# Dilated attention of a two-layer decoder trunk: one run of 64 steps per layer in place of two runs of 32

## What is computed

```python
def _dilated_attention(q, k, v):             # patterns (128, 1), (512, 4), (2048, 16)
    for window, dilation in DILATED_PATTERNS:
        o_i, lse_i = _dilated_branch(qp, kp, vp, window, dilation)
    ...
    w = jax.nn.softmax(jnp.stack(lses, axis=0), axis=0)
    o = jnp.einsum('gbsh,gbshd->bshd', w, jnp.stack(outs, axis=0).astype(jnp.float32))
...
mix = jnp.concatenate([attn, u], axis=-1)    # u: convolution of 31 taps, layernorm, silu
x = x + mix @ w_out[layer]
```

## Time and profile before

| | |
|---|---|
| median of 3 runs | 2617.43 us (2616.72 to 2618.36) |
| span of the profiled execution | 2619.3 us; the page gives no other time for it |
| PE, busy | 2491.9 us (95%) |
| DVE, busy | 1601.5 us (61%) |
| ACT, busy | 792.5 us (30%) |
| POOL, busy | 188.1 us (7%) |

### The profile page before, as it was taken

How to read it: one execution, slowest core, us unless ns; L and a number is a source line. 1 busy time by engine, 2 the same in 40 slices (tenths; PEclk the granted TensorE clock), 3 DMA queues, 4 the chain that set the end, 5 groups by cost and what they waited for, 6 DMA issues and landing times.

```text
span 2619.3 us, 33211 instructions
## 1 busy us (share of the span) xinstructions
PE 2491.9 (95%) x11824; PEld 2064.4 (79%) x11824; DVE 1601.5 (61%) x1490; ACT 792.5 (30%) x1037; POOL 188.1 (7%) x71
## 2 busy tenths in 40 slices
PE   6999889999999999999989997889999999999998
PEld 5878678778888888888778776787788888888887
DVE  5788867454555555555548897664465555555555
ACT  4222355333222222222332224553332222222221
POOL 1223100110000000000002330001100000000000
PEclk8999889999999999999989998999999999999999
DMA  3232631011111111111002226300111111111111
GB/s 120 63 90 72 177 89 48 24 41 49 49 49 48 48 48 48 48 48 48 32 34 73 80 80 185 89 24 32 41 49 48 48 48 48 48 48 48 48 48 72
DMA packets 46379, 159.29 MB, mean 61 GB/s; under 512 B 7392, under 2 KB 7776, under 8 KB 46304
## 3 DMA queue, kind: packets, MB, share of 16 engines
q1 hardware_dynamic: 45152, 154.12, 18.7%
q10 hardware_dynamic: 1152, 4.19, 0.4%
HBM read 133.12 MB, written 25.17 MB: 60 GB/s over the span
## 4 chain that ended last, share of the span: by engine, by line
PE 72%; DVE 13%; DVEq 7%; issue 3%; ACT 2%; DMA 1%; SPq 1%; ACTq 0%
PE mm L397 44%; PE aux L397 19%; DVE y L964 7%; PE aux L536 4%; PE aux L520 2%; DVEq L966 2%; PE mm L500 2%; DVE y L1118 1%; DVEq L1008 1%; DVEq L1120 1%; PE aux L421 1%; PE aux L573 1%; DVE o L1006 1%; DVEq L1001 1%; ACT x_hi L670 1%
## 5 line engine op out<-in xcount | busy, mean ns | idle before, releaser
L397 PE MATMUL mm<-x_hi,w_hi 128*128 128x512 f32 x2304 | 727.3, 397 | 34.7 <-DVE x_lo L937 17.0
L397 PE MATMUL mm<-x_lo,w_hi 128*128 128x512 f32 x2304 | 718.3, 393 | 0.0
L397 PE MATMUL mm<-x_hi,w_lo 128*128 128x512 f32 x2304 | 718.3, 393 | 0.0
L397 PEld LDWEIGHTS mm<-x_hi,w_hi 128*128 128x128 f32 x2304 | 434.9, 190 | 132.4 <-DVE x_lo L937 19.4
L397 PEld LDWEIGHTS mm<-x_lo,w_hi 128*128 128x128 f32 x2304 | 437.4, 190 | 96.1
L397 PEld LDWEIGHTS mm<-x_hi,w_lo 128*128 128x128 f32 x2304 | 436.6, 189 | 93.9
L647 ACT ACTIVATE w_hi<-w_raw 128x1024 fp32r<-128x1024 f32 x188 | 197.2, 1058 | 767.7 <-PE mm L397 576.2
L1133 DVE TENSOR_TENSOR x<-x,aux 128x1024 f32<-128x1024 f32 x176 | 214.8, 1220 | 136.4 <-PE aux L397 126.9
L931 DVE TENSOR_TENSOR w_lo<-w_raw,w_hi 128x1024 fp32r<-128x1024 f32 x188 | 228.2, 1222 | 38.3 <-ACT w_hi L647 25.1
L964 DVE SCALAR_TENSOR_TENSOR y<-u_pad,cpar,y (+1 forms) x152 | 210.8, 1387 | 26.2 <-issue 26.2
L943 DVE TENSOR_TENSOR uv<-mm,rinv 128x1024 f32<-128x1024 f32 x44 | 53.9, 1225 | 220.8 <-PE mm L397 220.5
(11 more groups left out here) (152 smaller groups left out, 2493.9 us busy)
## 6 DMA issues: line engine op xcount, KB each, us to landing
w_raw<-weights SPq DMA_DIRECT2D x188, 512.0 KB, 3.3
qk_scratch<-m SPq DMA_DIRECT2D x64, 128.0 KB, 2.1
qk_scratch<-o SPq DMA_DIRECT2D x64, 128.0 KB, 2.1
x_hi<-qk_scratch SPq DMA_DIRECT2D x32, 256.0 KB, 6.0
x<-xT ACTq DMA_DIRECT2D x8, 512.0 KB, 11.2
q_st<-qk_scratch SPq DMA_DIRECT2D x8, 512.0 KB, 3.5
k_hh<-qk_scratch SPq DMA_DIRECT2D x16, 256.0 KB, 5.7
k_ll<-qk_scratch SPq DMA_DIRECT2D x16, 256.0 KB, 6.1
```

Source lines behind the costliest of these rows:

```text
L397: last = pe.matmul(acc[:, cols], a, b[:, cols], start=start and n == 0, stop=stop and n == 2)
```

## The change

`STEPS` becomes `HEADS * TB` = 64, the loops over `i` go on all four engines, and the eight heads of a layer follow each other without a break. The fills are made for the whole layer: 104 in place of 2 x 52. Output turns come in steps 22, 38, 54 and 70 (`O_AT = 22`), in which they follow the attend of step n - 3; the first three lie in block 6 of heads 2, 4 and 6, where VectorE has no tap. In the output turn ScalarE now copies a bank twice, to `x_hi` and back over the half of `o_nat` that was just transposed, and the second copy frees the bank. VectorE waits for the bank's count and subtracts from that copy in `rinv`. The 44 taps are one list: six in each of heads 0 to 6 and two in head 7. SyncE fetches the values of pairs 2 and 3 at the starts of heads 4 and 6.

```diff
-TURN_HEADS = 4
-TURNS = HEADS // TURN_HEADS
-STEPS = TURN_HEADS * TB
+STEPS = HEADS * TB
+O_AT = 22
...
-    for n in range(STEPS + 6):
+    for n in range(STEPS + 7):
...
-        if n >= 21 and (n - 21) % (2 * TB) == 0:
+        if n >= O_AT and (n - O_AT) % (2 * TB) == 0:
             for half in range(2):
-                fills.append((n, "o", (n - 21) // (2 * TB), half, None))
+                fills.append((n, "o", (n - O_AT) // (2 * TB), half, None))
...
-                with sp.Fori(0, TURNS - 1) as i:
-                    for h in range(2, TURN_HEADS + 2):
-
-                        sp.wait_ge(mm_full, at(l, MM, M_SCORE + (h - 1) * TB, STEPS, i))
-                        load_head(h % 2, i * TURN_HEADS + h)
-                        if h >= TURN_HEADS:
-                            b = h - TURN_HEADS
-                            sp.wait_ge(step_done, at(l, HEADS * TB, (b + 1) * 2 * TB, STEPS, i))
-                            load_v(b, i * 2 + 2 + b)
...
+                for h in range(2, HEADS):
+
+                    sp.wait_ge(mm_full, at(l, MM, M_SCORE + (h - 1) * TB))
+                    load_head(h % 2, h)
+                    if h % 2 == 0 and h >= PAIRS:
+                        pair = h // 2
+                        sp.wait_ge(step_done, at(l, STEPS, (pair - 1) * 2 * TB))
+                        load_v(pair % 2, pair)
...
-                with pe.Fori(0, TURNS) as i:
...
-                with act.Fori(0, TURNS) as i:
...
-                            act.activation(x_hi[:, i * 2 + which, a * BANK:(a + 1) * BANK], bank, ACT.Copy
-                                           ).then_inc(o_hi, 1)
...
+                        act.activation(x_hi[:, which, a * BANK:(a + 1) * BANK], bank, ACT.Copy).then_inc(o_hi, 1)
+                        act.activation(o_nat[:, a * 4:(a + 1) * 4, :], bank.rearrange("p (b c) -> p b c", c=P),
+                                       ACT.Copy).then_inc(pt_read[f % 2], 1)
...
-                with dve.Fori(0, TURNS) as i:
...
-                        dve.wait_ge(o_hi, at(l, 2 * PAIRS, 2 * which + a + 1, 4, i))
-                        out = (slice(None), i * 2 + which, slice(a * BANK, (a + 1) * BANK))
-                        dve.tensor_tensor(x_lo[out], bank, x_hi[out].bitcast(F32), ALU.subtract
-                                          ).then_inc(pt_read[f % 2], 1)
-                        dve.drain().then_inc(o_split, 1)
...
+                    fills = [g for g in range(f + 1) if g % 2 == f % 2]
+                    dve.wait_ge(pt_read[f % 2], at(l, PT // 2, len(fills) + 1))
+                    out = (slice(None), which, slice(a * BANK, (a + 1) * BANK))
+                    dve.tensor_tensor(x_lo[out], rinv[:, a * BANK:(a + 1) * BANK], x_hi[out].bitcast(F32),
+                                      ALU.subtract)
+                    dve.drain().then_inc(o_split, 1)
...
-                    attn_taps = [(c, j) for c in range(CT // TURNS) for j in TAPS_ATTN]
+                attn_taps = [(c, j) for c in range(CT) for j in TAPS_ATTN]
```

More of the change, by code:

```diff
@@ L486, in _ @@
                 plain(pe)
-                with pe.Fori(0, TURNS) as i:
[L488 to L533, removed]
-                        out = stat_s[:, hh * BANK + qb * HEAD_DIM:hh * BANK + (qb + 1) * HEAD_DIM]
-                        for kb in range(qb + 1):
-                            last = pe.matmul(out, pT[n % 2][:, kb, :], vp[b][:, kb, hh * HEAD_DIM:(hh + 1) * HEAD_DIM],
-                                             start=kb == 0, stop=kb == qb)
-                        last.then_inc(step_done, 1)
-                    for n in range(STEPS + 6):
-                        if n < STEPS:
-                            scores(n)
-                        for f in range(PT_TURN):
-                            if FILLS[f][0] == n and FILLS[f][1] == "p":
-                                turn(f)
-                        if 3 <= n < STEPS + 3:
-                            attend(n - 3)
-                        for f in range(PT_TURN):
-                            if FILLS[f][0] == n and FILLS[f][1] == "o":
-                                turn(f)
@@ new lines, in scores @@
+                def scores(n):
+                    h, qb = n // TB, n % TB
+                    b = h % 2
+                    if qb == 0:
+                        pe.wait_ge(head_loaded[b], at(l, 80 * HEADS // 2, 80 * (h // 2 + 1)))
+                    pe.wait_ge(mm_read, at(l, MM, M_SCORE + n + 1))
+                    keys = (qb // 2 + 1) * 2 * P
+                    for a in range(0, keys, BANK):
+                        z = min(a + BANK, keys)
+                        for k in (k_hh, k_ll):
+                            last = pe.matmul(mm[n % 2][:, a:z], q_st[b][:, qb * P:(qb + 1) * P], k[b][:, a:z],
+                                             start=k is k_hh, stop=k is k_ll)
+                    last.then_inc(mm_full, 1)
@@ new lines, in attend @@
+                def attend(n):
+                    h, qb = n // TB, n % TB
+                    b, hh = h // 2 % 2, h % 2
+                    if n % (2 * TB) == 0:
+                        pe.wait_ge(v_loaded[b], at(l, 16 * PAIRS // 2, 16 * (h // 4 + 1)))
+                    if qb == 0:
+                        pe.wait_ge(o_read, at(l, HEADS, h + 1))
+                    for bank in range(2):
+                        fills = [f for f in range(LAST_FILL[n] + 1) if f % 2 == bank]
+                        pe.wait_ge(pt_read[bank], at(l, PT // 2, len(fills) + 1))
+                    out = stat_s[:, hh * BANK + qb * HEAD_DIM:hh * BANK + (qb + 1) * HEAD_DIM]
+                    for kb in range(qb + 1):
+                        last = pe.matmul(out, pT[n % 2][:, kb, :], vp[b][:, kb, hh * HEAD_DIM:(hh + 1) * HEAD_DIM],
+                                         start=kb == 0, stop=kb == qb)
+                    last.then_inc(step_done, 1)
@@ L553, in out_unit @@
+                for n in range(STEPS + 7):
+                    if n < STEPS:
+                        scores(n)
+                    for f in range(PT):
+                        if FILLS[f][0] == n and FILLS[f][1] == "p":
+                            turn(f)
+                    if 3 <= n < STEPS + 3:
+                        attend(n - 3)
+                    for f in range(PT):
+                        if FILLS[f][0] == n and FILLS[f][1] == "o":
+                            turn(f)
                 def out_unit(u, k0, midway=None):
```

155 lines of the change are left out of this document (83 added, 72 removed).

## The result

| | before | after |
|---|---|---|
| median, us | 2617.07 (2615.45 to 2618.36, 4 runs) | 2599.32 (2592.83 to 2602.67, 4 runs) |
| ratio | | 0.9925, 95% interval 0.9908 to 0.9941 |
| span of the profiled execution | 2619.3 | 2600.8 |

The change makes the kernel 17.8 us faster by the medians, 0.68%, which lies within the interval of the ratio. The prediction had the direction and less than half of the size: 8.5 us, 2608.9, with a range that ended at 2602.

A forecast was written before the change was run, and what follows sets the result against it. The prediction took the chain of waits, mostly matmuls, as the bound, with attention's output turns costing time over plain heads. Its sum, 33.3 + 0.7 - 21.0 - 4.5 = 8.5 us saved, gave 2608.9 us, range 2602 to 2618.

The forecast's parts named there:

- 33.3 us over plain heads: Attention, both layers: six two-head pieces together exceed the time of heads without an output turn (19.00 us each) by 33.3 us.
- X: Delay each new output turn adds to a two-head piece: 3.5 us, floor 2.1, ceiling 4.5; six make 21.0.
- the replay: New turn's order laid over head 1's trace: banks free at 330.9 and 332.0, next score read 4.5 us late.
- The clock term: Output turns: two of six lose the granted clock, costing 1.5 + 3.0 = 4.5 us; bounds 0 and 13.5.
- The stage's end: Last output turn: column sums start 0.4 us earlier because ScalarE's second copy frees the bank; 0.7 saved in two layers.
- The bound of 5.1 us: Head 7 loses two taps of 1.28 us: counted as 0, with bounds of 0 and 5.1 us saved.
- Everything else: Time outside the six pieces, the stages' ends and beginnings; the forecast had no term for it.
- the run's end: Middle piece of each layer: pipeline empties, output turn alone, refill; claimed gone with 64 steps in a row.
- the nearly absorbed turn: Rival, output turn: only VectorE's 2.1 us remain, 21.4 us saved, 2596.0 us; chance 0.07.
- The clock never falls: Rival, output turn: granted clock stays up in the new turn, 13.0 us saved, 2604.4 us; chance 0.17.
- The loss: Rival: 4.5 us delay stays whole at half clock, 6.75 a turn, 6.5 us lost, 2623.9; loss from 5.7; chance 0.10.
- The signs I named: Block 3 reads 41 to 43 us apart, score read 4 to 5 late, next head's block 1 about 3.5, clock mostly 1.00.

The follow-up runs named there:

- the second profile: The kernel before, unchanged, profiled once more: span 2614.7 us.
- three profiles: The changed kernel, unchanged, profiled three times: spans 2600.8, 2590.8 and 2597.9 us.
- the third copy: Changed kernel with ScalarE copying each half of an output turn once more, behind a drain, before freeing the bank: 2616.53 us, ratio 0.9998 to the kernel before.
- The early turn: Changed kernel with TensorE turning behind the next step's scores and ScalarE reading ahead of the exponential: 2588.4 us; with VectorE subtracting two steps later too, 2585.47.
- the old turn in one run: Changed kernel with ScalarE copying once and VectorE subtracting from the bank and freeing it; single run of 64 steps kept: 2596.82 us, ratio 0.9916.
- the taps dealt out as before: Changed kernel with convolution taps again 22 in heads 0 to 3 and 22 in heads 4 to 7: 2596.11 us, ratio 0.991.
- the subtractions later: Changed kernel with only VectorE's two subtractions of a turn done two steps later: 2592.47 us, ratio 0.9906.
- the scores twice: Changed kernel with the score matmuls behind each output turn inside the stage issued twice, to fill TensorE's wait: 2597.23 us, ratio 0.9917.

## Why the prediction fell short

Against the median of after, 2599.3, the forecast was 9.6 us too high. By its steps:

1. **33.3 us over plain heads** was read rightly (34.4 in the second profile), and the six pieces did become alike.
2. **X = 3.5 was 3.0.** A piece without a fall is 41.03. Up to VectorE the replay held: from the block 6 read, the first bank was to be free after 3.33 us and was after 3.36 (349.54 - 346.18), the second after 4.38 and was after 4.26, and the score read of block 7 was to be 4.5 late and was 4.3 (5.36 behind the block 6 read, where the plain head has 1.02). The stretch from the attend to the next head's block 1 failed: counted 3.75, it took 354.10 - 350.71 = 3.39. Of the 0.36, 0.14 is my rounding up ("335.95, say 336.1"). For the rest, from the attend to the transposes behind the wait the plain head takes 330.55 - 328.42 = 2.13 and this one 352.08 - 350.71 = 1.37: without its wait the stretch is 0.76 shorter, not the 0.61 that I took off. Six turns: 2.8 us too much.
3. **The clock term, 4.5 us, had the right count and the wrong price.** Of 18 turns in three profiles six lost the clock, 2 of 6 as forecast. But I priced each as in the old turn, where it lay behind the wait. Three of the six lay inside the turn, on time in which TensorE waits for the bank anyway, and were free; two cost 1.3 to 1.4; the one of 20.4 us cost 7.6. An execution so paid 7.6, 1.4 and 1.3 us: some 3.1 less than forecast in two of the three, 3.1 more in the first one. In the first pair of profiles the saving of the pieces, 7.5, agrees with the forecast of 33.3 - 25.5 = 7.8 only because this error cancels that of X.
4. **The stage's end, 0.7 us, was 3.8.** The turn's share was 1.3, part of it a fall that ran over the old turn's last transposes. The rest, 2.5, is the taps of head 7 (2 x 1.47, less a fall at the end of layer 1), which I counted at 0 "since TensorE's transposes and attends end that head". The reads show otherwise: from block 3 to block 7 of head 7 VectorE takes 7.87 us with four taps in that head and 457.10 - 450.06 = 7.04 with two, and the work behind gains as well. The bound of 5.1 us was there; the value within it was wrong. Some 3.1 us.
5. **Everything else** was taken as unchanged. It moved by 6.8 us in the first pair of profiles, along with the clock there, and lies within 10 us in all; how much of that belongs to the change is open.

2.8, 3.1 and 3.1 make 9.0 us, near the 9.6 by the medians, but that they close it so nearly is partly luck. In the first pair of profiles the span fell by 18.4 us, 9.9 more than forecast, and these are 3.1 from the end, 0.3 from the beginnings and 6.8 from everything else, less 0.3 from the pieces. What stands in every profile is X and the end, 5.9 us. The range joined the clock's bound with half of the taps' and left X at 3.5; three errors of the same sign, each within its bound, were more than that.

**What the gain is made of** was also told wrongly: all was said to hang on X, with the run's end gone. The old turn costs 2.9 us where its fall is hidden, the new one 3.0. What the pieces with a turn had above 40.88, 1.5 to 3.1 us each, goes with the clock, which fell behind the turn in every one of them and now falls in one of three, half of the times for nothing. (The old turn stood a step earlier, so 40.88 is not its own price there; the new turn takes 40.6 there at full clock.) The run's end was never seen without a fall of 6.8 us, so what an empty pipeline costs by itself stays open. That longer pauses of TensorE bring the falls back is shown by the third copy: with 0.7 us more in each of two pauses the clock fell in six of six turns, and the mean granted clock of the whole execution was 0.972 to 0.974 in all ten runs, against 0.977 to 0.981 in the runs of the changed kernel and 0.971 to 0.977 in the kernel before. The early turn has neither long pauses nor falls between steps. That the pauses alone decide is not shown: with those of the changed kernel the clock fell in 0 to 6 of six turns, each of the other kernels has one profile, and the six turns of one execution need not be independent trials. Which of the change's parts shortened what the clock sees is not shown: the old turn in one run has pauses of 1.55 and 1.49 us and falls in all six turns, but at a harmless place in five. Nor is it shown whether that comes from the single run or from the later step, which that kernel had together.

**The rivals.** In time the nearly absorbed turn came nearest, 2596.0, but not for its reason: X was 3.0 and not VectorE's 2.1, and doing VectorE's part later won only 0.3. In mechanism none was right: the clock did fall, on average in the two turns of six that the forecast had, and in two of three profiles at a third of its price. "The clock never falls", 2604.4, corrected by X and the end would be 2604.4 - 2.8 - 3.1 = 2598.5. The loss needed 5.7 us a piece. With the third copy the pieces hold 36.1 / 6 = 6.0, more than in the kernel before, and only the end, 37.0 in place of 39.5, brings the sum back to nothing.

**The signs I named** were weaker than I took them for. Pieces of 41 to 43, the read of block 7 late by 4 to 5 and X within 2.8 to 4.8 all came true, or nearly (the next head's block 1 was 3.0 late, not 3.5; one piece was above 44), and the time was still outside the range: none of them looks at the end of the stage or at where in the turn a fall lies.

## What to carry to other kernels

A wait on TensorE can have two prices, the wait itself and the clock behind it. Measure both by making the wait longer on purpose: here 0.7 us in each of two pauses turned a gain of 18 to 23 us into none, about half of it by the wait itself. Put the next step's matmuls ahead of a short piece of work that TensorE has to wait for, and let the engine that frees its bank do that first. A stretch at the lower clock is to be charged only where it covers work that somebody waits for, and work dealt out anew (here two taps) is to be priced in the stretch that loses it and in the one that gets it.

## What had not been expected of the hardware

The same pauses of TensorE gave very different numbers of falls. With 1.55 and 1.26 us the clock fell in 2, 3 and 1 of six turns of the changed kernel, in none with the taps dealt out as before, and in all six with the subtractions later, which leaves TensorE's order alone. With pauses up to 0.82 us (the turn early) it fell in 0 of 12, with one of 1.55 and one of at most 0.43 (the scores twice) in 0 of 6, with one of 1.92 (the third copy) in 6 of 6.

Once down behind a turn, the clock stayed for 3.4, 6.8, 10.2 or 20.4 us, and the longest of these went on without a pause: from 392.00 to 412.40 TensorE was busy for 20.40 of 20.40 us, with scores, transposes and attends, at a granted clock of 0.50 (shown ahead). The Trainium skill ("TensorE: Matmul & The Clock Gate", section "What's actually happening") has the clock throttled by default and released by activity. The falls behind pauses agree with the first half; that a TensorE without a pause stays at 1.2 GHz for 20 us is not what one reads from it, and what ended that stretch is open.
